# A decoder step with mixture of experts on one core: experts' lists behind the indices, the second pass's gate matrix in a free room, a first norm by channel blocks, router sums spread

## Chip, core and metric

The kernel runs on one core of one Trainium2 chip. The time is device microseconds (us) of one execution. The core's engines run side by side: PE (TensorE, matmuls), DVE (VectorE), ACT (ScalarE), POOL (GpSimd) and SP (SyncE, which here only issues transfers). They meet at semaphores. PE's clock has two levels, 2.4 and 1.2 GHz; the profile gives the granted share (1.00 and 0.50).

## What is computed

One decoder layer for a prompt (1024 tokens) and for samples (8 x 4 tokens), all float32, width 1024. What matters here is the end of the mixer and the whole of the channel mixer:

```python
def conv_module(glu_ext, w, b, ln_g, ln_b):
    y = lax.conv_general_dilated(...) + b                  # depthwise, width 31, 512 channels
    return jax.nn.silu(layernorm(y, ln_g, ln_b))           # norm over channels, then swish

xp = xp + g1p * mix_merge(att, cv, w_out[l])               # concat(att, cv) @ w_out

def moe(h, w_router, b_router, wg, wu, wd):                # 16 experts in 4 groups, top 2 of the best group
    logits = jnp.einsum('nd,de->ne', t, w_router)
    probs = jax.nn.softmax(logits, axis=-1)
    ...
    a = jnp.einsum('nd,edf->nef', t, wg)                   # gate: 1024 -> 512
    b = jnp.einsum('nd,edf->nef', t, wu)                   # up
    act = jax.nn.silu(a) * b * gates[:, :, None]
    return jnp.einsum('nef,efd->nd', act, wd)              # down: 512 -> 1024
```

Only chosen token rows go through an expert, 2112 rows in all.

## The kernel before

Every engine has a program written out by hand, and the order of the code is the order of the work; cross-engine waits are semaphores (`S["..."]`).

**The mixer's end.** Convolution and LayerNorm work in `cvT` (512 channels as 4 blocks `ch` of 128 partitions). Columns are normed in three groups j of up to 512 tokens. For j = 0: PE spreads the inverse deviation (`ln_spread`), DVE multiplies (`ln_scale`, line 2411), ACT takes four sigmoids, one a channel block (`ln_gate`, line 1309, each adds 1 to `ln_sig`), and DVE does scale and shift of the four blocks (line 2391) and the product with the sigmoids (line 2394) in `ln_swish`. Then PE may begin with the convolution's half of the output projection (`mix(0, 1)`, line 1793). DVE's order there: `ln_scale(0)`, two products of the modulation rows (line 2421, after 17 small transfers `mod2_in`), one tap of the last convolution, `ln_swish(0)`, two more taps.

**From there to the experts.** For each token tile t DVE merges the residual (`merged`, 2455 and 2458), norms (`normed`, 2478 and 2481, giving h2), PE transposes h2 (`route`, line 1835), multiplies with the router's weights (`router_strips`, 1846) and sums four strips (`router_sum`, 1853). Tile 8 holds the samples. The most frequent expert of the first tiles, the early expert, is calculated on PE in the meantime (`early_gate_or_up` 1894, `early_down` 1909). After the last `router_sum` DVE makes the routing: the choice (to `mask_ready`, line 2698), ranks from PE (1969 to 1973), the experts of the first pass (`zero_exp`), slots, the experts of passes 0 to 2 (`first_exp`), the number of pass pairs (`n_pairs`, 2832) and the experts of all passes (`experts_of(MT, pass_exp)`, 2767 to 2783). Then it adds up the early expert's rows (`early_combine`, 2624 and 2626), copies the weights of the slots, evacuates the upper half of the first pass's transposed rows (`turned_hi(0)`, 2839), and makes the indices of the later passes (`idx`, 2850 to 2874). PE turns positions into slots with `to_slots` (line 1983; three calls, each adds 1 to `slots_done`).

**Passes.** A pass has 128 rows in two halves x of 64, each half with an expert of its own. PE does, for pass t: second half of up, in between the transposes of the next pass's rows (2002), then the gate of pass t+1 (`gate_or_up`, 2011), the transposes of the activations (2018), and down (2025). Each matrix is 2 MB; gate, up and down have one buffer for each half x (`wg_sb`, `wu_sb`, `wd_sb`). SP refills a buffer once PE is through with it (`g_mm`, `u_mm`, `y_mm`), and leaves the load out if the half keeps its expert. So the gate matrix for pass 1 is issued only when the gate matmuls of pass 0 are done. Routing the reference's inputs gives for (lower, upper) half: early expert 15, pass 0 (15, 0), pass 1 (15, 7), pass 2 (15, 6); there are 18 passes. POOL gathers and scatters rows by indirect DMA.

Of the kernel before, what the change touches and what calls it, by code (L numbers as in the profile page):

```python
# [38 lines left out]
def decoder_step(nc, x_prompt, x_sample, cache_k, cache_v, state_conv, page_table, c_prompt, c_sample,  # L39
# [62 lines left out]
    with ctx:  # L102
# [259 lines left out]

        gate_row = low[:, 0:2 * D].rearrange("p (s n) -> p s n", s=2)
# [60 lines left out]
        wg_in = [sem(f"wg_in{i}") for i in range(2)]  # L424
        wu_in = [sem(f"wu_in{i}") for i in range(2)]
# [85 lines left out]
        def _(sp):  # L511
# [274 lines left out]
            for landed in e_w_in:  # L786
# [10 lines left out]
                         cond=e0[0] != held).then_inc(wd_in[0], 16)  # L797
            sp.wait_ge(S["g_mm"], 1)
            settle(sp)
            load_w(wg_sb, w_gate, wg_in, e1, e0)  # L800
# [3 lines left out]
            def refill(t, now, nxt, then):  # L804
# [5 lines left out]
                load_w(wg_sb, w_gate, wg_in, then, nxt)  # L810
# [4 lines left out]
            refill(0, e0, e1, e2)  # L815
# [619 lines left out]
        def _(pe):  # L1435
# [521 lines left out]
            early_gate_or_up(1, 0, 0, 3)  # L1957
            route(NTP)
            router_strips(NTP - 1)
            early_gate_or_up(1, 0, 3, 4)  # L1960
            router_sum(NTP - 1)
            router_strips(NTP)
            early_gate_or_up(1, 0, 4, 5)
            router_sum(NTP)
            early_gate_or_up(1, 0, 5, KD)
# [40 lines left out]
            def gate_or_up(s, w, k0, k1):  # L2006
                w_sb = (wg_sb, wu_sb)[w]
                for k in range(k0, k1):
                    for x in range(2):
                        half = slice(UR * x, UR * (x + 1))  # L2010
                        mm = pe.matmul(bank[half, 2 * s + w, :], xgT[:, s, k, half], w_sb[:, x, k, :],  # L2011
                                       start=(k == 0), stop=(k == KD - 1))
                if k1 == KD:
                    mm.then_inc(S[("g_mm", "u_mm")[w]], 1)
# [35 lines left out]
            def step(t, d, nth):  # L2050
# [9 lines left out]
                gate_or_up(1 - d, 0, 0, KD // 2)  # L2060
                pe.wait_ge(S["act_done"], t + 2)
                turn_act(d)
                gate_or_up(1 - d, 0, KD // 2, KD)
# [6 lines left out]
            step(0, 0, 1)  # L2070
# [49 lines left out]
        def _(dve):  # L2120
# [264 lines left out]
            def ln_swish(j):  # L2385
                c0, n = LN_COLS[j]
                y = cvT[:, :, c0:c0 + n]
                dve.wait_ge(S["ln_norm"], N0["ln_norm"] + j + 1)
                dve.wait_ge(S["ln_sig"], N0["ln_sig"] + NCH * (j + 1))
                for ch in range(NCH):  # L2390
                    c.put(V.tensor_scalar(cvT[:, ch, c0:c0 + n], cvT[:, ch, c0:c0 + n], cw[:, ch, CW + 1:CW + 2],
                                          cw[:, ch, CW + 2:CW + 3], ALU.mult, ALU.add))
                c.wait()
                V.tensor_tensor(y, y, ln_b[:, :, 0:n], ALU.mult).then_inc(S["ln_done"], 1)  # L2394
# [480 lines left out]
            dve.sem_inc(S["tok_ready"], 1)  # L2875
            pairs_used = dve.value_load(n_pairs[0:1, 0:1], min_val=1, max_val=MP // 2 - 1)
# [91 lines left out]
```

## Time and profile before

| | |
|---|---|
| median of 3 runs (lowest to highest) | 1221.47 us (1215.25 to 1223.01) |
| the profiled execution's own time | 1221.55 us |
| its span | 1219.8 us |
| PE busy, share of the span | 1151.7 us, 94% |
| DVE, ACT, POOL busy | 617.9, 339.5, 256.2 us |
| mean granted PE clock | 0.98 |
| chain that ended last: PE, DVE, DMA | 75%, 10%, 6% |

The span runs from the first to the last instruction; times in rows are microseconds from its start. PE is busy in almost all of it, so a time that PE waits, or works at the lower clock, is what a change can win. A wait in another engine matters only where PE waits for it.

### The profile page before, as it was taken

How to read it: one execution, taken by the hardware profiler on the slowest of the kernel's cores; microseconds unless marked ns; L12 is line 12 of the kernel's file. 1: busy time of each engine (PE TensorE's matmuls, PEld its weight loads, DVE VectorE, ACT ScalarE, POOL GpSimd, SP SyncE). 2: the span in 40 equal slices, each digit the busy share in tenths (PEclk: the TensorE clock that was granted, in tenths of full speed). 3: DMA queues.
4: the chain of work that ended last, by engine and by line, in shares of the span. 5: the costliest groups of instructions: out<-in, count | busy, mean ns of one | idle time of the engine just before them, and what ended most of it. 6: DMA issues, size and time to landing. Idle time of an engine off the chain costs nothing.

```text
span 1219.8 us, 19159 instructions
## 1 busy us (share of the span) xinstructions
PE 1151.7 (94%) x6692; PEld 541.3 (44%) x6692; DVE 617.9 (51%) x1255; ACT 339.5 (28%) x719; POOL 256.2 (21%) x303
## 2 busy tenths in 40 slices
PE   6999999999988999998999999879999989999995
PEld 3444444444445666666444454323333333333332
DVE  0010767786868999999865466612121112112121
ACT  2132221222127888888122322000000000000000
POOL 2011102220139910000100010202223322222222
PEclk8999999999998999999999999889999999999998
DMA  9943234232336474646341273769978697968984
GB/s 357 339 147 99 87 109 126 91 94 88 91 115 238 153 247 143 239 156 226 105 136 71 87 279 122 292 241 342 347 246 302 232 355 274 329 232 312 337 307 131
DMA packets 114100, 250.76 MB, mean 206 GB/s; under 512 B 14446, under 2 KB 28910, under 8 KB 113000
## 3 DMA queue, kind: packets, MB, share of 16 engines
q1 hardware_dynamic: 93345, 206.85, 48.7%
q0 software_dynamic: 16704, 38.30, 8.9%
q10 hardware_dynamic: 3984, 4.72, 1.2%
q8 instruction: 42, 0.69, 0.2%
q14 instruction: 25, 0.20, 0.1%
HBM read 370.93 MB, written 38.17 MB: 335 GB/s over the span
## 4 chain that ended last, share of the span: by engine, by line
PE 75%; DVE 10%; DMA 6%; issue 4%; SPq 3%; ACT 3%; POOL 0%; DVEq 0%; POOLq 0%; ACTq 0%
PE bank L1602 20%; PE bank L2011 20%; PE bank L2025 9%; PE bank L1793 7%; PE bank L1582 3%; DMA big<-in_w_gate_dram 3%; PE bank L1894 2%; DVE big L2291 2%; DVE cvT L2342 2%; DVE big L2301 2%; PE bank L1457 1%; PE bank L2002 1%; PE bank L1664 1%; DMA mid<-in_w_ada_dram 1%; PE bank L1636 1%
## 5 line engine op out<-in xcount | busy, mean ns | idle before, releaser
L2011 PE MATMUL bank<-big,mid 128*64 128x512 f32 x1120 | 258.3, 609 | 14.4 <-DMA big<-in_w_gate_dram 10.0
L1602 PE MATMUL bank<-big 128*128 128x512 f32 x560 | 249.2, 598 | 0.1
L1602 PEld LDWEIGHTS bank<-big 128*128 128x128 f32 x560 | 103.6, 190 | 131.3 <-issue 131.3
L2186 DVE SCALAR_TENSOR_TENSOR cvT<-low,cw,cvT 128x256 f32<-128x256 f32 x360 | 156.9, 511 | 0.0
L2011 PEld LDWEIGHTS bank<-big,mid 128*64 128x64 f32 x1120 | 79.6, 140 | 165.2 <-issue 164.9
L2025 PE MATMUL bank<-big,mid 128*64 128x512 f32 x544 | 119.6, 592 | 0.0
L2291 DVE TENSOR_TENSOR_SCAN big<-big 128x513 f32<-128x513 f32 (+4 forms) x96 | 91.6, 992 | 4.7 <-ACT big L1198 4.5
L2883 DVE TENSOR_TENSOR xt<-xt,bank 128x512 f32<-128x512 f32 x18 | 12.4, 688 | 145.7 <-ACT xt L1399 145.7
L2902 DVE TENSOR_TENSOR mid<-bank,low 128x512 f32<-128x512 f32 x34 | 21.9, 686 | 112.0 <-PE bank L2025 62.9
L889 POOL TENSOR_TENSOR st<-st,mhalf 128x16 f32<-128x16 f32 (+1 forms) x9 | 25.2, 2802 | 252.6 <-DVE st L2217 243.8
L2025 PEld LDWEIGHTS bank<-big,mid 128*64 128x64 f32 x544 | 39.1, 137 | 77.7 <-issue 77.7
L1394 ACT ACTIVATE mid<-bank 128x512 f32<-128x512 f32 x18 | 10.8, 598 | 185.9 <-PE bank L2002 175.2
L1793 PE MATMUL bank<-mid,cvT 128*128 128x512 f32 x128 | 59.9, 616 | 2.4 <-DVE cvT L2394 2.4
L1793 PE MATMUL bank<-mid,big 128*128 128x512 f32 x128 | 58.1, 597 | 0.0
L1198 ACT ACTIVATE big<-bank,nbb 128x512 f32<-128x512 f32 (+3 forms) x96 | 51.3, 596 | 5.2 <-PE bank L1636 3.6
L1664 PE MATMUL bank<-identf,big 128*128 128x128 f32 x288 | 44.8, 284 | 8.3 <-ACT mid L1231 4.2
L1211 ACT ACTIVATE big<-bank,bb 128x512 f32<-128x512 f32 (+3 forms) x96 | 52.1, 619 | 0.0
L1003 POOL DMA_INDIRECT out_dram<-mid,o_col x17 | 17.1, 1007 | 163.4 <-DVE mid L2904 163.4
L2301 DVE TENSOR_TENSOR big<-big 128x512 f32<-128x512 f32 (+3 forms) x96 | 51.1, 569 | 0.4
L2342 DVE SCALAR_TENSOR_TENSOR cvT<-low,cw,cvT 128x256 f32<-128x256 f32 x120 | 49.7, 479 | 0.0
L1083 ACT ACTIVATE big<-bank,low 128x128 f32<-128x128 f32 x64 | 23.4, 467 | 92.1 <-PE bank L1496 56.8
L1636 PE MATMUL bank<-big 64*128 64x512 f32 (+3 forms) x192 | 45.2, 549 | 3.2 <-ACT big L1211 2.0
(461 smaller groups left out, 1396.8 us busy)
## 6 DMA issues: line engine op xcount, KB each, us to landing
big<-in_w_gate_dram SPq DMA_DIRECT2D x39, 2048.0 KB, 9.3
big<-in_w_up_dram SPq DMA_DIRECT2D x37, 2048.0 KB, 8.3
big<-in_w_down_dram SPq DMA_DIRECT2D x37, 2048.0 KB, 13.8
low<-in_w_ada_dram SPq DMA_DIRECT2D x32, 512.0 KB, 4.2
low<-in_cache_v_dram SPq DMA_DIRECT2D x64, 256.0 KB
big<-in_w_in_dram SPq DMA_DIRECT2D x8, 1280.0 KB, 17.2
xt<-in_x_prompt_dram SPq DMA_DIRECT2D x16, 512.0 KB, 4.8
mid<-in_w_ada_dram SPq DMA_DIRECT2D x8, 1024.0 KB, 14.1
```

The costliest lines, as they stand in the source:

```text
L1198: nc.scalar.activation(keep[w][h][:, first:first + n], bank[:, 2 * (i % 2) + h, 0:n], ACT.Sigmoid, scale=-(HD ** -0.5), bias=nbb[:, 2 * pa ...
L1211: nc.scalar.activation(sig[w][h][:, b0 * P:b1 * P], bank[:, 2 * (i % 2) + h, 0:n], ACT.Sigmoid, scale=HD ** -0.5, bias=bb[:, 2 * pair + h: ...
L1602: mm = pe.matmul(bank[:, 4 if cc == 2 else cc, :], hT[:, s, k, :], w_in_sb[:, k, cc * 512:(cc + 1) * 512], start=(k == 0), stop=(k == KD - 1))
L1636: mm = pe.matmul(bank[:, 2 * (i % 2) + h, 0:n], stage[64 * h:64 * h + 64, s, 0, qb * P:(qb + 1) * P], stage[64 * h:64 * h + 64, s, 1, b0 * ...
L1664: mm = pe.transpose(bank[:, TURN_BANK["a", 2 * i + h], (kb - b0) * P:(kb - b0 + 1) * P], sig[u % 2][h][:, kb * P:(kb + 1) * P], identf[:, :])
L1793: mm = pe.matmul(bank[:, 2 * (t % 2) + cc, :], cat[:, k % NPAIR, t * P:(t + 1) * P], w_out_sb[:, k, cc * 512:(cc + 1) * 512], start=(k == ...
L2011: mm = pe.matmul(bank[half, 2 * s + w, :], xgT[:, s, k, half], w_sb[:, x, k, :], start=(k == 0), stop=(k == KD - 1))
L2025: mm = pe.matmul(bank[half, 6 + w, :], actT[:, s, k, half], wd_sb[:, x, k, w * 512:(w + 1) * 512], start=(k == 0), stop=(k == KF - 1))
L2186: c.put(V.scalar_tensor_tensor(out, src, cw[:, ch, tap:tap + 1], out, ALU.mult, ALU.add))
L2291: V.tensor_tensor_scan(kept, kept, kept, 1.0, ALU.mult, ALU.bypass).then_inc(S["scan_done"], 1)
L2301: V.tensor_tensor(sig[w][h][:, b0 * P:b1 * P], sig[w][h][:, b0 * P:b1 * P], keep[w][h][:, first + b0 * P:first + b1 * P], ALU.mult).then_i ...
L2342: c.put(V.scalar_tensor_tensor(out, x, cw[:, ch, tap:tap + 1], out, ALU.mult, ALU.add))
```

## The change

1. `ln_swish(0)` waits for the sigmoids one channel block at a time, and stands directly behind `ln_scale(0)`; the modulation rows' products and the tap that stood ahead of it come after it.
2. Between the last transposes and sums of the router PE does other numbers of early-expert matmuls: 1, 3, 3 and 1 steps where it did 3, 1, 1 and 3.
3. DVE: `experts_of(MT, pass_exp)` moves behind the indices, and `turned_hi(0)` ahead of the copies of the slots' weights. A fourth count of `tiles_ready` tells SP of the list.
4. The upper half's gate matrix of pass 1 is loaded into `wg_next`, a room in `low` that is free once the third `to_slots` is done, and not into `wg_sb`. PE's `step(0)` reads it there. The load has no condition.

```diff
+        SP0 = 9400 - KD * F
+        wg_next = low[:, SP0:].rearrange("p (k n) -> p k n", k=KD)
...
+            sp.wait_ge(S["slots_done"], N0["slots_done"] + 3)
+            sp.dma_start(wg_next, w_gate[0, bass.ds(e1[1], 1), :, :].rearrange("a (k p) n -> p (a k) n", p=P)).then_inc(wg_next_in, 16)
             sp.wait_ge(S["g_mm"], 1)
+            sp.sem_inc(wg_in[1], 16)
             settle(sp)
-            load_w(wg_sb, w_gate, wg_in, e1, e0)
+            sp.dma_start(wg_sb[:, 0, :, :], w_gate[0, bass.ds(e1[0], 1), :, :].rearrange("a (k p) n -> p (a k) n", p=P),
+                         cond=e1[0] != e0[0]).then_inc(wg_in[0], 16)
...
-            early_gate_or_up(1, 0, 0, 3)
+            early_gate_or_up(1, 0, 0, 1)
             route(NTP)
             router_strips(NTP - 1)
-            early_gate_or_up(1, 0, 3, 4)
+            early_gate_or_up(1, 0, 1, 4)
             router_sum(NTP - 1)
             router_strips(NTP)
-            early_gate_or_up(1, 0, 4, 5)
+            early_gate_or_up(1, 0, 4, 7)
             router_sum(NTP)
-            early_gate_or_up(1, 0, 5, KD)
+            early_gate_or_up(1, 0, 7, KD)
...
                 arrived(wg_in, 16 * t + 32)
-                gate_or_up(1 - d, 0, 0, KD // 2)
+                if gates is not None:
+                    pe.wait_ge(wg_next_in, 16)
+                gate_or_up(1 - d, 0, 0, KD // 2, gates)
...
-                dve.wait_ge(S["ln_sig"], N0["ln_sig"] + NCH * (j + 1))
                 for ch in range(NCH):
+                    dve.wait_ge(S["ln_sig"], N0["ln_sig"] + NCH * j + ch + 1)
                     c.put(V.tensor_scalar(cvT[:, ch, c0:c0 + n], ...))
...
             ln_scale(0)
+            ln_swish(0)
             dve.wait_ge(S["mod2_in"], N0["mod2_in"] + 16 * 17)
...
-            conv_tap(CW - 3)
-            ln_swish(0)
-            for tap in range(CW - 2, CW):
+            for tap in range(CW - 3, CW):
                 conv_tap(tap)
...
             op(V.tensor_copy(n_pairs[:, :], r_half))
-            experts_of(MT, pass_exp)
             dve.sem_inc(S["tiles_ready"], 1)
-            for j in range(NEB):
-                early_combine(j)
...
+            for j in range(NEB):
+                early_combine(j)
+            dve.wait_ge(S["xg_ps"], 1)
+            turned_hi(0)
             dve.wait_ge(S["slots_done"], N0["slots_done"] + 2)
             c.put(V.tensor_copy(w_slot[0:UR, :], bank[0:UR, 3, 0:MT]))
             c.put(V.tensor_copy(w_slot[UR:, 0:MB], bank[UR:, 3, 0:MB]))
-            dve.wait_ge(S["xg_ps"], 1)
-            turned_hi(0)
...
             dve.sem_inc(S["tok_ready"], 1)
+            experts_of(MT, pass_exp)
+            dve.sem_inc(S["tiles_ready"], 1)
```

DVE at the first norm, before (2411 is `ln_scale`, 2421 the modulation rows, 2342 taps, 2391 and 2394 `ln_swish`; the names in brackets are the semaphores by their first names, `sg_done` being `ln_sig`):

```order
L2411 TENSOR_TENSOR cvT<-cvT,bank 128x4x512 [waits st_ps]
L2421 SCALAR_TENSOR_TENSOR low<-low 128x1024 [waits qk_sq]
L2421 SCALAR_TENSOR_TENSOR low<-low 128x256
L2342 SCALAR_TENSOR_TENSOR cvT<-low,cw,cvT 128x256 [waits dve_c] x4
L2391 TENSOR_SCALAR cvT<-cvT,cw 128x512 [waits sg_done,mm_chunk]
L2391 TENSOR_SCALAR cvT<-cvT,cw 128x512 x3
L2394 TENSOR_TENSOR cvT<-cvT,big 128x4x512 [waits dve_c]
L2342 SCALAR_TENSOR_TENSOR cvT<-low,cw,cvT 128x256 [waits dve_c] x8
```

And now (line numbers of the changed kernel: 2424, 2404, 2407, 2435, 2355):

```order
L2424 TENSOR_TENSOR cvT<-cvT,bank 128x4x512 [waits st_ps]
L2404 TENSOR_SCALAR cvT<-cvT,cw 128x512 [waits sg_done,mm_chunk]
L2404 TENSOR_SCALAR cvT<-cvT,cw 128x512 [waits sg_done] x3
L2407 TENSOR_TENSOR cvT<-cvT,big 128x4x512 [waits dve_c]
L2435 SCALAR_TENSOR_TENSOR low<-low 128x1024 [waits qk_sq]
L2435 SCALAR_TENSOR_TENSOR low<-low 128x256
L2355 SCALAR_TENSOR_TENSOR cvT<-low,cw,cvT 128x256 [waits dve_c] x12
```

The two products and four tap instructions have gone behind the norm's five, and the four scalings wait one by one.

PE at the end of the router, before (1894 early expert's gate, 1835 `route`, 1846 strips, 1853 sums; the rows with 128x2 and 32 are the samples' tile):

```order
L1853 MATMUL bank<-strip_sum,big 128x16
L1894 MATMUL bank<-big 128x512 x7
L1835 MATMUL bank<-identf,low 128x128 x2
L1846 MATMUL bank<-big,wr 16x128 x8
L1894 MATMUL bank<-big 128x512
L1853 MATMUL bank<-strip_sum,big 128x16
L1846 MATMUL bank<-big,wr 16x32 x8
L1894 MATMUL bank<-big 128x512
L1853 MATMUL bank<-strip_sum,big 32x16
L1894 MATMUL bank<-big 128x512 x11
```

And now:

```order
L1863 MATMUL bank<-strip_sum,big 128x16
L1904 MATMUL bank<-big 128x512 x5
L1845 MATMUL bank<-identf,low 128x128 x2
L1856 MATMUL bank<-big,wr 16x128 x8
L1904 MATMUL bank<-big 128x512 x3
L1863 MATMUL bank<-strip_sum,big 128x16
L1856 MATMUL bank<-big,wr 16x32 x8
L1904 MATMUL bank<-big 128x512 x3
L1863 MATMUL bank<-strip_sum,big 32x16
L1904 MATMUL bank<-big 128x512 x9
```

The samples' transposes come 2 matmuls of the program earlier, and the last sum 2 later. (The profile shows two instructions for each matmul of the program.)

SP's transfers at the same place now (804 is the load into the free room, 808 and 811 the gate's other half, `s_o_ps` is `slots_done`):

```order
L801 DMA big<-in_w_down_dram 128x4x1024 [waits late_in2]
L804 ISA [waits s_o_ps]
L804 DMA low<-in_w_gate_dram 128x8x512
L808 REGISTER_ALU [waits g_mm]
L808 REGISTER_ALU
L808 ISA
L811 TENSOR_LOAD n_pairs [waits tiles_ready]
```

The load that stood behind `g_mm` now stands ahead of it; nothing else was moved on SP.

## Rows read from the trace of the kernel before

**Rows 1.** Waits of PE, the largest row: us in total, times, longest.
```profile
PE bank L2011 <- DMA big<-in_w_gate_dram: 10.0, 2, 6.2
```
**Rows 2.** Timeline of PE at the first norm: start, us, what, [idle before].
```profile
589.84 8.75 PE L1793 MATMUL bank<-mid,big 128*128 128x512 f32 x20
601.03 15.70 PE L1793 MATMUL bank<-mid,cvT 128*128 128x512 f32 x32 [2.44 <-DVE cvT L2394]
...
620.86 1.04 PE L1835 MATMUL bank<-identf,low 128*128 128x128 f32 x8
```
**Rows 3.** Timeline of DVE at the first norm.
```profile
593.68 1.56 DVE L2421 SCALAR_TENSOR_TENSOR low<-low 128x1024 f32<-128x1024 f32 x2 [1.35 <-DMA low<-in_norm_ffn_dram]
...
596.75 1.91 DVE L2391 TENSOR_SCALAR cvT<-cvT,cw 128x512 f32<-128x512 f32 x4
598.69 2.29 DVE L2394 TENSOR_TENSOR cvT<-cvT,big 128x2048 f32<-128x2048 f32 x1
...
609.97 1.22 DVE L2455 TENSOR_TENSOR low<-bank,low 128x1024 f32<-128x1024 f32 x1 [1.07 <-PE bank L1793]
...
615.89 1.22 DVE L2481 TENSOR_TENSOR low<-low 128x1024 f32<-128x1024 f32 x1
```
**Rows 4.** Line 1309, ACT's sigmoids: duration ns min/median/max, first and last start.
```profile
L1309 ACT ACTIVATE big<-cvT,cw x4: 797/799/813, 592.4 to 594.5; 128x512 f32<-128x512 f32 x4
```
**Rows 5.** Window: length, PE, PEld, DVE, ACT, POOL busy, PEclk, DMA share, GB/s.
```profile
602.00:604.00 2.00, 2.00 (x4) 0.81 (x3) 2.00 (x6) 0.00 (x0) 0.00 (x0) 0.50 0.03 8
```
**Rows 6.** Timeline of PE from the router's end to pass 1.
```profile
730.02 6.25 PE L1894 MATMUL bank<-big 128*128 128x512 f32 x14
...
739.63 9.71 PE L1894 MATMUL bank<-big 128*128 128x512 f32 x22
749.17 0.23 PE L1969 MATMUL bank<-big,identb 128*128 128x160 bf16 x1
...
773.03 2.94 PE L1983 MATMUL bank<-low 128*64 128x40 f32 x108
780.30 13.40 PE L2011 MATMUL bank<-big,mid 128*64 128x512 f32 x48 [4.33 <-DVE mid L2839]
...
804.47 6.40 PE L2011 MATMUL bank<-big,mid 128*64 128x512 f32 x16 [6.16 <-DMA big<-in_w_gate_dram]
```
**Rows 7.** Timeline of DVE from the samples' h2 to the indices.
```profile
735.53 0.42 DVE L2481 TENSOR_TENSOR low<-low 128x256 f32<-128x256 f32 x1
...
748.05 0.37 DVE L2698 TENSOR_TENSOR r_maskb<-mid 128x128 bf16<-128x128 f32 x2
...
769.22 1.29 DVE L2767 TENSOR_TENSOR mid<-mid 128x640 f32<-128x640 f32 x2
...
773.62 0.27 DVE L2783 CAST pass_exp<-mid 128x40 int32<-128x40 f32 x2
...
777.93 1.23 DVE L2626 TENSOR_TENSOR cvT<-cvT,low 128x1024 f32<-128x1024 f32 x1
...
779.50 0.69 DVE L2839 COPY mid<-bank 128x512 f32<-128x512 f32 x1
```
**Rows 8.** Chain that ended last: start, us, what.
```profile
780.30 9.99 PE bank L2011 x32
791.12 13.21 DMA big<-in_w_gate_dram
...
826.37 7.02 PE bank L2011 x32
...
973.97 17.35 DMA big<-in_w_gate_dram
```
**Rows 9.** SP's issue of pass 0's gate matrix.
```profile
759.38 0.40 SPq L780 DMA_DIRECT2D big<-in_w_gate_dram  x1
```
**Rows 10.** Windows while pass 0's matrices land (columns as in rows 5).
```profile
776.00:778.00 2.00, 0.00 (x0) 0.00 (x0) 1.97 (x4) 0.00 (x0) 0.44 (x1) 1.00 1.03 408
...
782.00:784.00 2.00, 2.00 (x8) 0.79 (x6) 0.96 (x6) 0.00 (x0) 0.00 (x0) 0.50 0.32 125
```

More of the change, by code:

```diff
@@ L361, in decoder_step @@
         y_t = mid[:, 6144:8192].rearrange("p (s n) -> p s n", s=2)
+        SP0 = 9400 - KD * F
+        wg_next = low[:, SP0:].rearrange("p (k n) -> p k n", k=KD)
+        assert SP0 >= 4 * D
         gate_row = low[:, 0:2 * D].rearrange("p (s n) -> p s n", s=2)
@@ L424, in decoder_step @@
         wg_in = [sem(f"wg_in{i}") for i in range(2)]
+        wg_next_in = sem("wg_next_in")
         wu_in = [sem(f"wu_in{i}") for i in range(2)]
@@ L797, in _, with refill @@
                          cond=e0[0] != held).then_inc(wd_in[0], 16)
+            sp.wait_ge(S["slots_done"], N0["slots_done"] + 3)
+            sp.dma_start(wg_next, w_gate[0, bass.ds(e1[1], 1), :, :].rearrange("a (k p) n -> p (a k) n", p=P)).then_inc(wg_next_in, 16)
             sp.wait_ge(S["g_mm"], 1)
+            sp.sem_inc(wg_in[1], 16)
             settle(sp)
-            load_w(wg_sb, w_gate, wg_in, e1, e0)
+            sp.dma_start(wg_sb[:, 0, :, :], w_gate[0, bass.ds(e1[0], 1), :, :].rearrange("a (k p) n -> p (a k) n", p=P),
+                         cond=e1[0] != e0[0]).then_inc(wg_in[0], 16)
             sp.wait_ge(S["tiles_ready"], 3)
             pairs_used = sp.value_load(n_pairs[0:1, 0:1], min_val=1, max_val=MP // 2 - 1)
-            def refill(t, now, nxt, then):
+            def refill(t, now, nxt, then, gates=None):
                 sp.wait_ge(S["u_mm"], t + 1)
@@ L809, in refill @@
                 settle(sp)
-                load_w(wg_sb, w_gate, wg_in, then, nxt)
+                load_w(wg_sb, w_gate, wg_in, then, gates or nxt)
                 sp.wait_ge(S["y_mm"], 2 * t + 6)
@@ L813, in refill @@
                 load_w(wd_sb, w_down, wd_in, nxt, now)
-            refill(0, e0, e1, e2)
+            refill(0, e0, e1, e2, (e1[0], e0[1]))
+            sp.wait_ge(S["tiles_ready"], 4)
             with sp.Fori(0, MP // 2) as i, sp.If(i < pairs_used):
@@ L2004, in turn_x, with gate_or_up @@
                 mm.then_inc(S["xg_ps"], 1)
-            def gate_or_up(s, w, k0, k1):
+            def gate_or_up(s, w, k0, k1, held=None):
                 w_sb = (wg_sb, wu_sb)[w]
+                held = held or (w_sb[:, 0, :, :], w_sb[:, 1, :, :])
                 for k in range(k0, k1):
@@ L2010, in gate_or_up @@
                         half = slice(UR * x, UR * (x + 1))
-                        mm = pe.matmul(bank[half, 2 * s + w, :], xgT[:, s, k, half], w_sb[:, x, k, :],
+                        mm = pe.matmul(bank[half, 2 * s + w, :], xgT[:, s, k, half], held[x][:, k, :],
                                        start=(k == 0), stop=(k == KD - 1))
@@ L2048, in _, with step @@
             pairs_used = pe.value_load(n_pairs[0:1, 0:1], min_val=1, max_val=MP // 2 - 1)
-            def step(t, d, nth):
+            def step(t, d, nth, gates=None):
                 arrived(wu_in, 16 * t + 16)
@@ L2059, in step @@
                 arrived(wg_in, 16 * t + 32)
-                gate_or_up(1 - d, 0, 0, KD // 2)
+                if gates is not None:
+                    pe.wait_ge(wg_next_in, 16)
+                gate_or_up(1 - d, 0, 0, KD // 2, gates)
                 pe.wait_ge(S["act_done"], t + 2)
                 turn_act(d)
-                gate_or_up(1 - d, 0, KD // 2, KD)
+                gate_or_up(1 - d, 0, KD // 2, KD, gates)
                 pe.wait_ge(S["aT_sb"], t + 1)
@@ L2068, in step @@
                 down(d, 1)
-            step(0, 0, 1)
+            step(0, 0, 1, (wg_sb[:, 0, :, :], wg_next))
             with pe.Fori(0, MP // 2) as i, pe.If(i < pairs_used):
```

## The prediction

> **What bounds it now.** First the table of busy times: PE works in 94% of the span, and the chain that ended last is three quarters PE. So I look for the places where PE stands still, in the list of its waits; its top row is the load of gate matrices, 10.0 us in two waits [rows 1]. The timelines then give the place, and show what a total hides, that matmuls after a wait are slower. Three waits touch this change.
>
> (a) At 601.03 PE has waited 2.44 us for `ln_swish(0)` [rows 2]. Before, 20 instructions took 8.75 us, 0.44 each; the 32 after it took 15.70, where 14.0 would do. The granted clock reads 0.50 at 602 to 604 [rows 5]: the lower level of 1.2 GHz, after an engine that stood still. The wait costs 2.44 + 1.7 = 4.1 us.
>
> (b) At 780.30 PE has waited 4.33 us for DVE's line 2839, `turned_hi(0)` [rows 6]. The first gate then takes 9.99 us for 32 instructions, a later one 7.02 [rows 8]: 2.97 for the clock, 0.50 in the window at 782 [rows 10]. Together 7.3 us.
>
> (c) At 804.47 PE has waited 6.16 us for the gate matrix of pass 1 [rows 6]; its 16 instructions then take 6.40, half of 7.02 is 3.51: 2.9 for the clock. Together 9.1 us. The load went out when the first gate was done and took 13.21 us [rows 8].
>
> The second gate wait, 10.0 - 6.16 = 3.8 us, is that behind the 17.35 us load at 973.97 [rows 1, 8]. Its load is issued by the loop, as now, and all that leads to it moves along, so I leave it.
>
> **The norm.** Sigmoids start from 592.4 to 594.5 and take 0.80 each [rows 4], so the last ends at 595.3. Now DVE takes each block as it comes; the last scaling, 0.54 (four in 1.91), ends at 595.9, and the product of 2.29 [rows 3] at 598.2. PE ends what it has at 589.84 + 8.75 = 598.6 [rows 2]: with 0.4 us to spare the wait and the drop of the clock both go, -4.1.
>
> What is late next? DVE still has the two products (1.56) and twelve tap instructions; the order is other, the work the same. It gave back 1.35 us of waiting for the modulation rows [rows 3] and takes up some 0.8 for the first sigmoid and the gaps between four, while the product and scalings come no slower; I put its free time at 0.5 us later than before. Before it was free 1.07 before `merged(0)` at 609.97 [rows 3], so `merged(0)` starts at about 609.4, 0.5 earlier though PE is 4.1 earlier. Tile 0's h2 then ends at 617.1 - 0.5 = 616.6 [rows 3]; PE gets to the transposes that need it at 621.0 - 4.1 = 616.9 [rows 2]. It just holds; PE keeps its 4.1. If the taps are some tenths longer, PE loses these tenths, and at worst (DVE moves nothing forward) the whole gain is gone. I take -4.1, bounds 0 and -4.4.
>
> **The sums.** Here I expect a loss. PE's timeline shows no wait from 730 to 776, so each wait put in there is paid in full. Before it did 7 steps of the early expert, 14 instructions in 6.10 us or 0.44 each, up to 736.3, and the samples' h2 came at 735.53 + 0.42 = 735.95 [rows 6, 7]: just in time. Now it does 5 steps and arrives 4 x 0.44 = 1.7 us earlier, at 734.5, while nothing brings h2 forward: PE waits 1.45. From there to the last sum stand the same small parts and 6 steps where 2 stood: it ended at 739.7 [rows 6], and now at 739.7 + 1.45 - 1.75 + 4 x 0.87 = 742.7 or so, some 2.9 later. DVE's choice hangs on it: its mask, at 748.4 [rows 7], comes at 751.3. PE has fewer steps left, and arrives at the ranks (before at 749.3 [rows 6]) at 749.3 + 1.45 = 750.8, so it waits 0.5 more. Sum 1.95, +2.0. The bound below is 0, if h2 comes earlier; above, 2.9, DVE's whole delay, if PE has no spare work. I take no drop of the clock for waits shorter than the 2.44 us of (a); if there is one, it is up to 1.7 more.
>
> **The lists.** `experts_of(MT, ...)` holds DVE from 769.22 to 773.9 [rows 7], ahead of the early sums. Without it the chain of DVE up to 769.2, moved by 2.2 (the first slots come 2.0 later from PE), ends at 771.4; the two early sums, 773.9 to 779.2 before [rows 7], take some 2.5 each, the second not before PE's early down matmuls, which ended before the transposes ahead of 773.03 (772.1, now 774.1), so to 776.6; `turned_hi(0)` takes 0.69 [rows 7]: 777.4. PE ends its slots at 773.03 + 2.94 = 776.0, now 778.0 [rows 6]. So PE does not wait, by 0.6 us: -4.33 and -2.97, with the +2.0 of the sums counted above. The list's 4.7 us now lie behind the indices (some 3 us of small instructions from 778), up to about 786. DVE's next work for PE, the gate's product, can start when gate 0 ends at 785 and its sigmoid is taken; nobody waits for it before the up matmuls are done at 793. SP needs the list only after the refills of `step(0)`.
>
> **The free room.** Gate 0 then runs from 778.0 to 785.0. From its start to PE's arrival at gate 1 it was 798.31 - 780.30 = 18.0 us, without the slow clock 15.0: PE arrives at 793.0. The room's load is issued at 778.1. In front of it in SP's queue are pass 0's three matrices, issued from 759.38 [rows 9] and, hanging on the routing, now 2.9 later. The engines of DMA were full (408 GB/s in the window at 776) and ran empty near 782.7 [rows 10], so now near 785.5. 2.1 MB at 400 GB/s take 5.3 us: 790.8 at the earliest. In that stretch POOL gathers the residual's rows, gate rows and rows of pass 2, 0.5 MB each: 1 to 1.5 MB more, 2.5 to 4 us, so 793.3 to 794.8. The nearest row from the other side is the longest load of a full stretch, 17.35 [rows 8]: 778.1 + 17.35 = 795.5. Between them I take 794.5: PE waits 1.5 us, and as 2.44 us cost 1.7 by the clock, I add 1.5. Of (c) that leaves -6.16 - 2.9 + 3.0 = -6.1; bounds -9.1 (in time) and -3 (landing at 797.5).
>
> The Trainium skill, page DMA: Bandwidth & Descriptors, section Queues, rings and completion order, says that each DMA engine takes turns between the queues that have work, and works through one queue in order. By that, the room's load cannot overtake pass 0's matrices, and halves its rate while POOL's gathers run. It speaks against hiding this load, and my 794.5 has the same sense; with the order of queues but without gathers it would be 790.8, and the sum 3.0 us less. No row here shows single queues at work.
>
> **The sum** against the profiled execution's 1221.55: -4.1 + 2.0 - 7.3 - 6.1 = -15.5, so 1206.0. The median, 1221.47, is the same within 0.1.
>
> **Rivals.**
> *In time.* The room's matrix is there at 793.0: three less, 1203.0; with h2 earlier, and so nothing lost in the sums, 1201. For it: DMA had run empty before gate 0's end [rows 10]. Against: the gathers. 0.18.
> *Late as before.* The last of the 16 DMA engines decides, and PE waits some 4 to 6 us with the clock's 3: -9.1 becomes -1, and the time 1210 to 1213. For it: the old load took 13.2 us though 2.1 MB need 5.3. Against: it goes out 12 us earlier. 0.08.
> *The norm brings nothing*, since DVE was the next bound all along: DVE's 0.5 us instead of 4.1, so 1209.6. For it: the 0.3 us margin at the first transposes. Against: DVE waited for PE at 609.97. 0.12.
> *The passes do not start earlier*: another waited-for thing, say pass 0's gate matrix, issued 2.9 later, holds gate 0 at 780. It must land by 778.0, 15.7 us after its issue at 762.3; as first in its queue it should take 8 to 10. Then the 4.33 and part of the clock stay: 1211 to 1213. 0.05.
> *Slower.* One mechanism: the room's load, put among pass 0's loads and the gathers, lands very late. The rest of the change is worth 18.5 us (15.5 + 3.0), and a landing L us after 793.0 costs L + 3. It turns to a loss for L over 15.5, a landing after 808.5, 30 us after its issue; over 1% slower after 820.7. The longest load seen took 17.35. 0.02.
>
> **Range and chances.** The forecast, 1203.5 to 1209, has 0.55. I reach down to 1200 for "in time" with the free sums, and up to 1213 for the late load and the lost norm. A measurement here tells about 1% from no change; faster by it is below 1209.3. Of the forecast and "in time" all lies there (0.73), of the rest a third: faster 0.80, same 0.18, slower 0.02.
>
> **What would show it.** In the changed profile: no PE wait before the convolution's half near 598.6, with 32 instructions in 14.0; all later places 4 earlier. At the samples' transposes a new PE wait of 1.4 for DVE's h2, and one of 0.5 before the ranks. Gate 0 starts straight after the slots, near 774 (778.0 - 4.1), and takes 7.0; its clock reads 1.00. Gate 1 starts near 790.5, after a wait of 0 to 3 us for the load into `low`. Wrong would be: a wait for DVE at the first transposes (then the norm's gain is lost), a wait for DVE or a DMA before gate 0, or a wait over 4 us before gate 1.

## The result and the profile after

| | before | changed |
|---|---|---|
| median, lowest to highest | 1220.0 us, 1215.25 to 1223.01 (4 runs) | 1202.4 us, 1199.41 to 1203.99 (4 runs) |
| the profiled execution's time and span | 1221.55, 1219.8 us | 1201.27, 1199.4 us |
| PE busy, mean granted clock | 1151.7 us, 0.98 | 1143.6 us, 0.99 |

The ratio is 0.9874, with an interval of 0.9851 to 0.9897: the change takes 12.6 to 18.2 us off, 15.4 by the ratio's middle and 17.6 by these medians. In a later comparison the changed kernel came to 1204.23 us against 1218.08, a ratio of 0.9894 (0.9845 to 0.9943). Forecast were 1206.0 us, a gain of 15.5. The pair of profiled executions differs by 20.4 us in span, more than the medians do; the end of this section shows where that comes from.

Lines of the changed kernel stand 10 or 11 further down on PE and ACT and mostly 12 or 13 on DVE (1793 is now 1803, 2011 is 2022, 2481 is 2493; `turned_hi`, 2839, is 2848). The list of PE's waits (us in total, times, longest) is the first thing to compare with [rows 1]:

```profile
PE bank L2022 <- DMA big<-in_w_gate_dram: 1.9, 1, 1.9
PE bank L1845 <- DVE low L2493: 1.7, 1, 1.7
...
PE bank L1979 <- DVE r_maskb L2710: 0.9, 1, 0.9
```

The 10.0 us for gate matrices have become 1.9, and two waits for DVE are new, 1.7 and 0.9. Now the same places in order of time, in PE's timeline after the change (start, us, what, [idle before]). They answer to [rows 2, 6]:

```profile
590.07 8.75 PE L1803 MATMUL bank<-mid,big 128*128 128x512 f32 x20
598.65 13.90 PE L1803 MATMUL bank<-mid,cvT 128*128 128x512 f32 x32
...
616.68 1.06 PE L1845 MATMUL bank<-identf,low 128*128 128x128 f32 x8
...
732.12 0.44 PE L1845 MATMUL bank<-identf,low 128*128 128x128 f32 x2 [1.74 <-DVE low L2493]
...
747.97 0.24 PE L1979 MATMUL bank<-big,identb 128*128 128x160 bf16 x1 [0.85 <-DVE r_maskb L2710]
...
771.99 2.90 PE L1993 MATMUL bank<-low 128*64 128x40 f32 x107
...
774.76 10.49 PE L2022 MATMUL bank<-big,mid 128*64 128x512 f32 x47
...
786.21 4.08 PE L2022 MATMUL bank<-big,mid 128*64 128x512 f32 x17
789.70 0.59 PE L2022 MATMUL bank<-low,mid 128*64 128x512 f32 x1
```

Read it as a lead, the start in before less the start after:

| place | before | after | lead, us |
|---|---|---|---|
| first transposes of h2 | 620.86 | 616.68 | 4.2 |
| ranks | 749.17 | 747.97 | 1.2 |
| last slots | 773.03 | 771.99 | 1.0 |
| gate of pass 0 | 780.30 | 774.76 | 5.5 |
| gate of pass 1 | 804.47 | 789.70 | 14.8 |
| down of pass 0 | 814.87 | 797.29 | 17.6 |
| late gate of pass 9 | 991.45 | 971.82 | 19.6 |

The norm brings 4.2; 3.1 of it are lost between the first transposes and the slots; the lists bring 4.5 at once, and 2.9 more while the gate of pass 0 runs at 2.4 GHz (47 instructions in 10.49 where 48 took 13.40 [rows 6]). At the gate of pass 1 the wait of 6.16 is gone, and its slow clock with it: 9.1 (from a lead of 8.5 at the end of gate 0 to 17.6). Here PE reads `low`, the free room, without any wait. The step from 17.6 to 19.6 and on to the 20.4 of the span is at a place that the change doesn't touch, the gate of pass 9. Before:

```profile
991.45 5.08 PE L2011 MATMUL bank<-big,mid 128*64 128x512 f32 x16 [3.88 <-DMA big<-in_w_gate_dram]
```

After:

```profile
971.82 3.65 PE L2022 MATMUL bank<-big,mid 128*64 128x512 f32 x16 [1.85 <-DMA big<-in_w_gate_dram]
...
986.80 3.65 PE L2022 MATMUL bank<-big,mid 128*64 128x512 f32 x16 [0.28 <-DMA big<-in_w_up_dram]
```

Wait and clock cost 2.0 and 1.4 us less there in this pair, against 0.3 for a new wait. That is not the change's doing: an execution of the same changed kernel, from the later comparison (label e9_changed_again), has 3.70 of wait and 6.64 of matmuls at this gate:

```profile
973.13 6.64 PE L2022 MATMUL bank<-big,mid 128*64 128x512 f32 x16 [3.70 <-DMA big<-in_w_gate_dram]
```

Over all profiles taken the wait lies between 1.85 and 4.52 us and the 16 instructions take 3.65 to 6.64, with no order by kernel. Wait and instructions together take 5.50 us in the first execution of the changed kernel and 10.34 in the second. So at this one place PE gains or loses some 5 us by chance, about as much as the runs of one kernel differ.

### The profile page after: what moved, and what is told of

It reads as the page before. It is cut to its first block, busy times and chain, and to the rows that moved or that the text cites. A ratio compares the mean times of both kernels' runs of the same rounds, so it can differ in the third digit from the quotient of the medians.

```text
span 1199.4 us, 19161 instructions
## 1 busy us (share of the span) xinstructions
PE 1143.6 (95%) x6692; PEld 540.0 (45%) x6692; DVE 618.3 (52%) x1255; ACT 339.4 (28%) x719; POOL 256.3 (21%) x303
## 4 chain that ended last, share of the span: by engine, by line
PE 68%; DVE 11%; DMA 9%; issue 6%; ACT 3%; SPq 2%; POOL 0%; POOLq 0%; DVEq 0%; ACTq 0%
PE bank L1612 21%; PE bank L2022 16%; PE bank L2036 7%; PE bank L1803 7%; DMA low<-out_dram,o_col 3%; PE bank L1592 3%; DVE big L2304 2%; DMA out_dram<-mid,o_col 2%; DVE big L2314 2%; PE bank L1467 2%; DVE cvT L2355 2%; DMA big<-in_w_up_dram 1%; PE bank L1674 1%; PE bank L2012 1%; DMA h_d<-low 1%
## 5 line engine op out<-in xcount | busy, mean ns | idle before, releaser
L2022 PE MATMUL bank<-big,mid 128*64 128x512 f32 x1104 | 251.1, 595 | 2.1 <-DMA big<-in_w_gate_dram 1.9
L2036 PE MATMUL bank<-big,mid 128*64 128x512 f32 x544 | 119.6, 592 | 0.0
```

Source lines behind the costliest of these rows:

```text
L2036: mm = pe.matmul(bank[half, 6 + w, :], actT[:, s, k, half], wd_sb[:, x, k, w * 512:(w + 1) * 512], start=(k == 0), stop=(k == KF - 1))
```

## The experiments

The theory after the first result: the change is four parts whose gains lie at four different places of PE, three of them as forecast (norm, lists, room), and one a loss (sums). The rival is that one of them carries the rest, or that a gain put down to a part is chance. So each part was done alone, then the losing part was undone, and its cause removed. Each comparison is with the kernel before on the same chip.

### The norm alone

```diff
-                dve.wait_ge(S["ln_sig"], N0["ln_sig"] + NCH * (j + 1))
                 for ch in range(NCH):
+                    dve.wait_ge(S["ln_sig"], N0["ln_sig"] + NCH * j + ch + 1)
...
             ln_scale(0)
+            ln_swish(0)
...
-            conv_tap(CW - 3)
-            ln_swish(0)
-            for tap in range(CW - 2, CW):
+            for tap in range(CW - 3, CW):
```

> The kernel before with the first norm's edit alone. The theory that the parts add up: PE starts the convolution's half without a wait, its 32 instructions take 13.9 us, and everything behind is 4.2 us earlier up to the experts; time -4.2 (ratio 0.9966). The rival that the norm only shifts a wait to the next stage says: PE waits for h2 at its first transposes or later, and before gate 0 the lead is under 1 us; time within 1 us of before.

Measured: 1215.2 us (1212.09 to 1221.56, 10 runs) against 1217.4 (21 runs), ratio 0.9983 (0.9963 to 1.0002). PE in its timeline:

```profile
599.37 13.90 PE L1793 MATMUL bank<-mid,cvT 128*128 128x512 f32 x32
...
776.95 12.15 PE L2011 MATMUL bank<-big,mid 128*64 128x512 f32 x48 [4.32 <-DVE mid L2838]
...
799.11 6.15 PE L2011 MATMUL bank<-big,mid 128*64 128x512 f32 x16 [5.40 <-DMA big<-in_w_gate_dram]
```

The wait at the norm is gone, the other two are where they were. Gate 0 starts 3.4 us earlier than in the kernel before; this execution was 0.9 us late already ahead of the norm (590.78 for 589.84 [rows 2]), so the norm's own part there is 4.3. PE still waits 4.32 for DVE before gate 0, so DVE's chain has moved forward with PE. The median is 2.2 less, with an interval from nothing to 4.5. So the gain is passed on whole as far as gate 0; in the end time about half of it is seen, and the interval touches both no change and all of it.

### The sums alone

```diff
-            early_gate_or_up(1, 0, 0, 3)
+            early_gate_or_up(1, 0, 0, 1)
...
-            early_gate_or_up(1, 0, 3, 4)
+            early_gate_or_up(1, 0, 1, 4)
...
-            early_gate_or_up(1, 0, 4, 5)
+            early_gate_or_up(1, 0, 4, 7)
...
-            early_gate_or_up(1, 0, 5, KD)
+            early_gate_or_up(1, 0, 7, KD)
```

> The kernel before with the other numbers of early-expert steps between the router's sums alone. Theory that this edit costs: PE waits 1.5 to 1.8 us for the samples' h2 and under 1 us for the mask, the last sum comes 3 us later, and gate 0, which DVE's chain releases here, starts 2.5 to 3 us later: time +2.8. Rival, that the edit is free because PE has 4.3 us to spare before gate 0 in this kernel: +0. Rival, that it gains because the sums no longer press ACT and DVE: -1.

Measured: 1219.9 us (1213.12 to 1223.03, 10 runs) against 1217.4, ratio 1.0022 (1.0001 to 1.0043): slower, by 0.1 to 5.2 us. PE:

```profile
736.42 0.44 PE L1835 MATMUL bank<-identf,low 128*128 128x128 f32 x2 [1.47 <-DVE low L2481]
...
752.26 0.24 PE L1969 MATMUL bank<-big,identb 128*128 128x160 bf16 x1 [0.85 <-DVE r_maskb L2698]
...
783.38 11.96 PE L2011 MATMUL bank<-big,mid 128*64 128x512 f32 x48 [4.16 <-DVE mid L2839]
```

Both new waits are there without any other part, and gate 0 starts 3.1 us later than in the kernel before, of which 0.4 came in ahead of the sums (the convolution's half starts at 601.42 for 601.03 [rows 2]). So the sums cost 2.7 here. The ranks come 2.7 later too, with 2.3 of it in the two waits. Gate 0 is still released by DVE (a wait of 4.16), so PE's spare time there doesn't absorb the loss: DVE's choice hangs on the last sum and comes later as well.

### The lists alone

```diff
             op(V.tensor_copy(n_pairs[:, :], r_half))
-            experts_of(MT, pass_exp)
             dve.sem_inc(S["tiles_ready"], 1)
...
+            dve.wait_ge(S["xg_ps"], 1)
+            turned_hi(0)
             dve.wait_ge(S["slots_done"], N0["slots_done"] + 2)
...
+            experts_of(MT, pass_exp)
+            dve.sem_inc(S["tiles_ready"], 1)
```

Not shown are SP's wait for the fourth count of `tiles_ready` and the old places of `early_combine` and `turned_hi(0)`.

> The kernel before with the list of all passes behind the indices (and the turned rows ahead of the slots' weights) alone. Parts add up: PE does not wait before gate 0, the clock stays at 1.00 there, and gate 0's 32 instructions take 7.0 us: -7.3. The wait for gate 1's matrix stays at 6 us with its slow clock, since the load still waits for gate 0. Rival, that the load is bound by traffic and not by its issue: with gate 0 earlier, the load meets more of pass 0's transfers, the wait at gate 1 grows to 8 us or more and gives back a third: -5.

Measured: 1206.85 us (1203.34 to 1211.46, 5 runs) against 1217.4, ratio 0.9919 (0.989 to 0.9948), a gain of 6.3 to 13.4 us. PE does not wait before gate 0, which starts at 773.68, 6.6 us earlier; 2.1 of that was there at the first transposes already (618.74 for 620.86 [rows 2]), ahead of this part, since the clock didn't fall at the norm in this execution (last section). So the lists' own part at gate 0 is 4.5. At gate 1 PE waits less, not as long or longer:

```profile
791.66 5.12 PE L2012 MATMUL bank<-big,mid 128*64 128x512 f32 x16 [2.88 <-DMA big<-in_w_gate_dram]
```

The load is still issued behind gate 0, but takes 9.91 us where it took 13.21. POOL's timeline shows what else was in flight. In the kernel before, the load ran from 791.1 to 804.3, and three gathers were issued around or in it:

```profile
789.43 1.01 POOL L998 DMA_INDIRECT low<-out_dram,o_col  x1 [1.77 <-DMA low<-out_dram,o_col]
...
791.42 0.99 POOL L979 DMA_INDIRECT mid<-h_d,x_col  x1 [0.79 <-issue]
...
795.88 0.97 POOL L979 DMA_INDIRECT mid<-h_d,x_col  x1 [0.80 <-POOL x_col L976]
```

With the lists alone it ran from 781.6 to 791.5, with two gathers issued beside it and the next ones as it ended or behind it:

```profile
782.77 1.06 POOL L991 DMA_INDIRECT low<-out_dram,o_col  x1 [0.92 <-POOL o_col L985]
784.13 0.96 POOL L993 DMA_INDIRECT low<-g_d,o_col  x1 [0.30 <-issue]
791.17 1.01 POOL L999 DMA_INDIRECT low<-out_dram,o_col  x1 [6.08 <-DMA low<-out_dram,o_col]
...
793.17 0.99 POOL L980 DMA_INDIRECT mid<-h_d,x_col  x1 [0.79 <-POOL x_col L977]
```

That both go together is shown; that the gathers made the 3.3 us is a reading, not tested by itself. There is a second candidate: the up matrices' loads were issued at 798.50 in the kernel before, 5.8 us before the gate matrix was there, and at 788.97 here, 2.6 us before.

### The free room alone

```diff
+            sp.wait_ge(S["slots_done"], N0["slots_done"] + 3)
+            sp.dma_start(wg_next, w_gate[0, bass.ds(e1[1], 1), :, :].rearrange("a (k p) n -> p (a k) n", p=P)).then_inc(wg_next_in, 16)
             sp.wait_ge(S["g_mm"], 1)
...
+                if gates is not None:
+                    pe.wait_ge(wg_next_in, 16)
+                gate_or_up(1 - d, 0, 0, KD // 2, gates)
```

> The kernel before with the free room alone. Parts add up: the wait of 6.2 us before gate 1 and 2.9 us of slow clock go, the wait of 4.3 us before gate 0 and its slow clock stay: -9.1. Rival, that most of the gain of the changed kernel came from the lists and the room only keeps the traffic apart: a wait of 2 us or more for the load stays, -6 or less. The load into the room should land near 789 to 790, some 8 us before PE needs it at 798.3.

Measured: 1211.02 us (1204.95 to 1217.68, 5 runs) against 1217.4, ratio 0.9932 (0.9905 to 0.9959), a gain of 5.0 to 11.6 us. Its profiled execution is the slowest of the five, and shows why it can be:

```profile
779.55 11.85 PE L2021 MATMUL bank<-big,mid 128*64 128x512 f32 x48 [4.33 <-DVE mid L2851]
...
868.40 6.63 PE L2021 MATMUL bank<-big,mid 128*64 128x512 f32 x16 [4.77 <-DVE mid L2851]
```

At gate 1 there is no wait any more; the load, issued at 775.40, took 13.2 us to land, so it was there at 788.6, as expected. The wait before gate 0 stays, since the room has nothing to do with it. But at 868.40 a wait appears that no other profile has. DVE's timeline tells it:

```profile
864.79 1.29 DVE L2914 TENSOR_TENSOR mid<-bank,low 128x512 f32<-128x512 f32 x2 [14.69 <-DMA low<-out_dram,o_col]
866.11 1.23 DVE L2916 TENSOR_TENSOR mid<-mid,low 128x1024 f32<-128x1024 f32 x1
867.25 0.68 DVE L2851 COPY mid<-bank 128x512 f32<-128x512 f32 x1
```

DVE has to add up a pass with rows that POOL gathered, the gather waited for the scatter of the pass before, and behind the sum on DVE stands the upper half of the next pass's rows, which PE's gate needs. In the kernel before DVE idles 9.22 and 9.77 us for this gather in two passes, without PE being held; here it was 14.69, and PE stood for 4.77.

### The changed kernel without the new sums

The theory of a loss is put to the test from the other side: the changed kernel, with the four counts of the early expert's steps (3, 1, 1, 3) as before. The changed kernel ran beside it.

```diff
-            early_gate_or_up(1, 0, 0, 1)
+            early_gate_or_up(1, 0, 0, 3)
...
-            early_gate_or_up(1, 0, 1, 4)
+            early_gate_or_up(1, 0, 3, 4)
...
-            early_gate_or_up(1, 0, 4, 7)
+            early_gate_or_up(1, 0, 4, 5)
...
-            early_gate_or_up(1, 0, 7, KD)
+            early_gate_or_up(1, 0, 5, KD)
```

> The changed kernel once more, as the measure for the three kernels beside it: 15 to 18 us under before (ratio 0.986 to 0.988). PE waits 1.7 us for the samples' h2 and 0.9 us for the mask, and none before gate 0 and gate 1. Differences to the first execution in the passes (a wait for weights or for DVE near pass 9 or passes 2 to 4, 0 to 6 us) would say that there the time varies from run to run.

> The changed kernel with the sums' edit undone (3, 1, 1, 3 steps again). Theory that the sums' edit loses: no wait at the samples' transposes nor before the ranks, gate 0 starts 2.9 us earlier against the kernel's start; the load into the room is issued 2.9 us earlier too, so gate 1 still finds it, or waits under 1 us. Time 2 to 3 us under the changed kernel. Rival, that DVE or the load then becomes the bound and takes the 3 us back before gate 0 or gate 1: no difference.

Measured: the changed kernel again 1204.23 us (1201.88 to 1210.94, 4 runs), ratio 0.9894 (0.9845 to 0.9943). Its trace has the two waits as 1.35 and 0.85, and none before gate 0 and gate 1. Without the new sums 1200.3 (1198.95 to 1202.62, 4 runs), ratio 0.9856 (0.9819 to 0.9892). Neither new wait is in its trace, gate 0 follows the slots at once:

```profile
770.92 10.49 PE L2022 MATMUL bank<-big,mid 128*64 128x512 f32 x47
```

From the start of the convolution's half (597.62 in this trace) to here are 173.3 us; with the new sums 175.7 and 176.1 in its two executions. So the sums cost 2.4 to 2.8 us inside the changed kernel. The load into the room moves along (issued at 772.31, for 775.12 with the new sums), and gate 1 doesn't wait here either. The medians are 3.9 apart; the intervals overlap.

### The store of h2 put first

Why does the samples' h2 come so late that a wait takes its place? DVE's row in the changed kernel names a transfer:

```profile
731.12 0.48 DVE L2490 SCALAR_TENSOR_TENSOR low<-low,st 128x256 f32<-128x256 f32 x1 [5.88 <-DMA h_d<-low]
```

It writes where the h2 of tile 6 lay, whose store stands on SP's queue behind the early expert's up and down matrices; the chain that ended last has this store:

```profile
716.36 14.65 DMA h_d<-low
```

Theory: not DVE is late, but a store that stands behind a load of 4 MB. The store was put ahead of the load, once with the new sums and once with the old:

```diff
                         sp.wait_ge(landed, EARLY)
+                    store_h2(t)
                     load_early_expert((1, 2))
-                store_h2(t)
+                else:
+                    store_h2(t)
```

> The changed kernel with SP's store of tile 6's h2 issued ahead of the early expert's up and down matrices (4 MB) and not behind them. If the samples' h2 is late because DVE waits for that store before it may write the buffer, DVE's wait of 5.9 us there shrinks to under 1, h2 is there 4 to 5 us earlier, and PE's waits of 1.7 and 0.9 us go: 3 us under the changed kernel. Rival, that the row sums of the samples' tile bound h2: DVE still waits, for POOL's root, and PE keeps over 1 us of its wait; no difference in time.

> The changed kernel with the store first and the sums' edit undone. If PE is the bound from the router to gate 0, this is as the kernel with the store first and the new sums, within 1 us in gate 0's start: with h2 early the place of the sums does not matter. If DVE's choice is the bound, the new sums with the early store are better, by up to 3 us, since there the last sum can come earlier.

Measured: with the new sums 1198.57 us (1196.38 to 1200.51, 4 runs), ratio 0.9834 (0.9797 to 0.9871); with the old sums 1199.74 (1195.56 to 1206.58, 4 runs), ratio 0.9854 (0.9801 to 0.9907). DVE in the first of them:

```profile
724.56 0.48 DVE L2492 SCALAR_TENSOR_TENSOR low<-low,st 128x256 f32<-128x256 f32 x1 [0.66 <-PE bank L1847]
```

The samples' h2 is there 5.2 us earlier, counted from the start of the convolution's half (598.65 in the changed kernel, 597.32 here), and PE has one wait left of the two, that before the ranks:

```profile
744.68 0.24 PE L1981 MATMUL bank<-big,identb 128*128 128x160 bf16 x1 [0.85 <-DVE r_maskb L2712]
```

From the convolution's half to gate 0 it takes 174.2 us with the new sums and 173.0 with the old. So the store is the cause of PE's wait for h2, 1.20 to 1.74 us in the executions with the new sums; this is shown. And even with h2 early the new sums lose 1.2 us to the old, which neither side of the last expectation said: the last sum ends later with them, the mask with it, and PE waits. This pair is also the one case of a single wait: the ranks come 1.0 us later (147.4 after the convolution's half for 146.4) for a wait of 0.85. By the medians the three kernels (without sums, store first, both) can't be told apart; each beats the changed kernel's median of the same comparison, by 3.9, 5.7 and 4.5 us. The four runs of store first with the new sums (at most 1200.51) don't overlap with the changed kernel's four beside them (at least 1201.88), but they do with its first four (from 1199.41). Up to gate 0 the store's order is worth 1.5 to 1.9 us by the traces (and 0.3 with the old sums, 173.3 to 173.0); what the median shows beyond that is not accounted for by it.

The Trainium skill, page DMA: Bandwidth & Descriptors, section Queues, rings and completion order, says that a DMA engine works through one queue in order. The 14.65 us of a store of 0.5 MB behind 4 MB, and its being gone when the order is turned, agree with it.

### The norm's place without the waits for single blocks

The last part of the norm: how much is the place, how much the waits block by block? The changed kernel with one wait for all four sigmoids, in the new place:

```diff
+                dve.wait_ge(S["ln_sig"], N0["ln_sig"] + NCH * (j + 1))
                 for ch in range(NCH):
-                    dve.wait_ge(S["ln_sig"], N0["ln_sig"] + NCH * j + ch + 1)
```

> The changed kernel with one thing undone: the blocks' scalings on VectorE wait for all four sigmoids again (in the new place, ahead of the product), not each for its own. It tells how much of the norm's 4.18 us is the place and how much the waits for single blocks. Theory: in the trace of the changed kernel the scalings wait 0.95, 0.16 and 0.16 us for single sigmoids; with one wait for the last of them the first scaling starts at about the last sigmoid's end, so the product ends about 1 us later, the 32 matmuls start at about 599.5 instead of 598.65 (against the first transposes' time), TensorE waits for them 0.5 to 1 us where it did not wait, and the transposes of h2 move later by 0.7 to 1 us: the place is worth over 3 of the 4.18 us. Rival: the single waits are what counts, the matmuls start where those of the kernel before do (601.0 with a wait of 2.44) and the transposes lose 2 us or more. The whole time is not told from the changed kernel's by either.

Measured with one run, 1202.79 us, which says nothing on this part; the trace does. PE:

```profile
599.86 14.00 PE L1803 MATMUL bank<-mid,cvT 128*128 128x512 f32 x32 [1.11 <-DVE cvT L2407]
...
618.00 1.09 PE L1845 MATMUL bank<-identf,low 128*128 128x128 f32 x8
```

PE waits 1.11 us again, the clock does not fall, and the transposes are 2.9 us ahead of the kernel before instead of 4.2. So the place is worth 2.9 and the single waits 1.3 (3.0 and 1.4 if counted from the 20 instructions ahead, which start at 590.00 here, 590.07 in the changed kernel and 589.84 before). That is nearer to the theory than to its rival, with a place worth a little less than the 3 that it gave and a start 0.4 later.

## Why the prediction was right, point by point

**The norm** (forecast -4.1): -4.2 in the profiled pair (4.4 counted from the 20 instructions ahead), in the step that was named, the wait of 2.44 and the 1.7 of the slow clock. Also the next step held: DVE's `merged(0)` starts at 609.44 (609.4 was worked out) and PE gets to the first transposes without a wait, so the rival that DVE takes the gain back is out. It was close: DVE ends tile 0's h2 at 616.59 and PE begins at 616.68, a margin of 0.1, where 0.3 was worked out (with 621.0 for the row's 620.86 [rows 2]; with the row it is 0.2).

**The sums** (forecast +2.0): 3.1 in the profiled pair, above the bound of 2.9, and 2.4 to 2.8 by the comparisons in the experiments, so 0.4 to 1.1 more than the sum had. The two waits were named; they are 1.74 and 0.85 where 1.45 and 0.5 were worked out. The second was added up wrong: 739.7 + 1.45 - 1.75 + 4 x 0.87 is 742.9, 3.2 later and not 2.9, and by that the wait would have been 0.8. The rest, 0.5 us beyond the waits (0.15 of it falls behind the ranks), was no term of the sum. I read the greater part so: at a wait the matmuls ahead of it run out and the next begins afresh, so what adjoining matmuls overlap is lost, some 0.2 us at each break. The one pair with a single break bears out the size: with the store first, the ranks come 1.0 us later for a wait of 0.85. The reason given for it is argued. No drop of the clock followed either wait.

**The lists** (forecast -7.3): -4.5 and -2.9, so 7.4 in the profiled pair, and DVE is through with `turned_hi(0)` (at 774.37) before PE is with the slots, as worked out. That the size fits so well is luck in part, for the sum took the clock's part from the same execution against which the pair measures it: the 48 instructions took 13.40 us after the wait there, but 12.15, 11.96 and 11.85 in the three other executions with a wait of 4.2 to 4.3 us. The part for the clock is 1.4 to 2.9, not 2.97 each time.

**The free room** (forecast -6.1): -9.1. This is the mis-sized term. I had the load land at 794.5, on the scale without the norm's 4.1 us, so 790.4, and took 3.0 us of wait and clock off the gain. Its issue in SP's timeline:

```profile
775.38 0.37 SPq L804 DMA_DIRECT2D low<-in_w_gate_dram  x1
```

By the trace's list of DMA issues it landed 13.5 us later. So it went out 1.4 us later than forecast (774.0), took 13.5 us where 16.4 were forecast, and was there at 788.9. The windows of the changed kernel (length, busy time of PE, PEld, DVE, ACT, POOL, PE's clock, DMA's share, GB/s) show the same:

```profile
786.00:788.00 2.00, 2.00 (x13) 0.69 (x13) 0.69 (x1) 0.60 (x1) 0.27 (x1) 1.00 0.98 341
788.00:790.00 2.00, 2.00 (x12) 0.69 (x10) 0.00 (x0) 0.00 (x0) 0.01 (x1) 1.00 0.44 160
790.00:792.00 2.00, 2.00 (x12) 0.72 (x10) 0.75 (x1) 0.00 (x0) 1.20 (x3) 1.00 0.10 18
```

The share falls to 0.44 in the window at 788 and 0.10 in the next, and PE, which comes at 789.70, doesn't wait. I had counted three kinds of gathers of POOL against the load, 2.5 to 4 us. POOL's timeline:

```profile
782.81 0.23 POOL L994 COPY o_col<-idx 128x3 int32<-128x3 int32 x1 [7.22 <-DMA out_dram<-cvT,eo_col]
783.95 1.05 POOL L1000 DMA_INDIRECT low<-out_dram,o_col  x1 [0.92 <-POOL o_col L994]
785.31 0.96 POOL L1002 DMA_INDIRECT low<-g_d,o_col  x1 [0.30 <-issue]
789.99 1.01 POOL L1008 DMA_INDIRECT low<-out_dram,o_col  x1 [3.71 <-DMA low<-out_dram,o_col]
```

Only two gathers were issued before the load was done. POOL itself waited 7.22 us for its scatter of the early rows, which was in the same full stretch, and the rest came at 789.99 and later. What was missing in my reading is that POOL's gathers hang on transfers of their own: here the scatter before them was slow to land in the full stretch, so the gathers came later and got out of the load's way. The load landed some 2.2 us after the 786.7 worked out without any gather, which is what two gathers of 0.5 MB take at 400 GB/s by the forecast's own sum (2.5), and 1.5 before my value. That this is why the load was early is argued; no run moved the gathers alone. The rival "in time" was the right one for this term. PE's margin is under 1 us.

**The sum.** By the places the four parts are worth 17.6 us in the profiled pair, 2.1 more than forecast: 3.0 more for the room, 0.2 for norm and lists, less 1.1 for the sums. Two errors of opposite sign thus partly cancel. That the ratio's middle gives 15.4, almost the forecast's 15.5, is chance; its interval of 12.6 to 18.2 holds both values. One chance was added up loosely as well: 0.73 and a third of the remaining 0.27 are 0.82, not 0.80.

**What was left out.** The late gate of pass 9: I had called it untouched, which it is, but it brought 3.2 us to the profiled pair. Wait and 16 instructions took 8.96 us in the kernel before, 5.50 in the first changed execution and 7.70 to 10.46 in the nine others, so against these the pair's gain there would have been 1.3 at most and a loss of 1.5 at worst. A profile's longest wait of its kind that comes and goes belongs in the range, at 2 to 4 us to either side. The single parts needn't add up either. By their ratios they are 2.1 + 9.9 + 8.3 - 2.7 = 17.6, and the whole is 15.4 and 12.9 in its two comparisons, with intervals too wide (5 to 7 us for the lists and the room) to call that a difference. By their mechanisms they overlap, since with the lists alone 3.3 of the 6.16 us wait, for which the room was made, are gone already.

**The rivals.** "The norm brings nothing" and "the passes do not start earlier" are out by the waits that don't stand ahead of the transposes and of gate 0; "late as before" and "slower" by the room's load being there. The chance on a gain over 1% was borne out by the first comparison (at least 1.0%, at most 1.5%); the second, 0.9894 (0.9845 to 0.9943), reaches under it.

## What to carry to other kernels

Work out a wait with what PE loses after it, and take the clock's part as a range from nothing to what one trace shows. When matmuls are moved to fill waits, ask which input comes late for the new place and why: here a store behind 4 MB in a queue. Turning the two took that wait away, while spreading the sums only lost. A load can be issued ahead of the work that frees its old buffer if some other room is free, and other engines' gathers in the same stretch need not stand against it in full, if they wait for transfers themselves; that last point is argued from one place here.

## What the runs showed of the hardware that was not expected

**What a wait costs by the clock varies between executions of the same instructions.** The 32 matmuls after the norm took 15.70 us after waits of 2.44, 2.31 and 2.08 (before, sums alone, room alone), but 14.00 after one of 2.31 with the lists alone:

```profile
600.61 14.00 PE L1794 MATMUL bank<-mid,cvT 128*128 128x512 f32 x32 [2.31 <-DVE cvT L2395]
```

The windows over them show the granted clock, 0.50 in the first (sums alone) and 1.00 in the second (lists alone); columns as above.

```profile
602.00:604.00 2.00, 2.00 (x4) 0.91 (x3) 2.00 (x6) 0.00 (x0) 0.00 (x0) 0.50 0.04 8
```

```profile
602.00:604.00 2.00, 2.00 (x6) 0.95 (x5) 1.75 (x6) 0.00 (x0) 0.14 (x1) 1.00 0.00 0
```

So after two waits of 2.31 us in the same place the clock read 1.2 GHz in one execution and 2.4 in the other. After the longer waits of this document the instructions behind them were slower every time: by 1.4 to 2.9 us at gate 0, by 1.5 to 2.8 at gate 1 (16 instructions in 5.12 to 6.40 us after waits of 2.88 to 6.38, for 3.65 at 2.4 GHz), and by 1.4 to 3.0 at pass 9 (5.08 to 6.64 after waits of 2.35 to 4.52). The length of the wait doesn't order these costs: 1.4 after 3.88 us and 1.7 after 2.35. Waits of 1.11, 1.74 and 1.85 us cost nothing by it.

**A second chain runs beside PE.** In the last passes the chain that ended last is not PE's. Its pieces in the changed kernel:

```profile
1103.28 5.54 DMA out_dram<-mid,o_col
...
1109.73 2.33 DMA low<-out_dram,o_col
...
1116.92 7.91 DMA low<-out_dram,o_col
1124.85 1.30 DVE mid L2915 x2
1126.17 1.24 DVE mid L2917
```

Scatter, gather and sum of a pass hang on those of the pass before, and one round, from 1124.85 to the next at 1148.11, takes 23.3 us where PE's pass takes 22.5 (downs at 1092.55 and 1115.06); the next, to 1168.54, takes 20.4. With the room alone this chain held PE for 4.77 us. In the profiled pair it took nothing visible from the gain: PE's last stage starts 28.7 us before the end of the span in the kernel before (1191.15) and 28.8 in the changed one (1170.61). Whether a further gain at the front would be lost to it was not tried.
